# Thirty-two tokens' activations from gathered rows stand in the gate table, and each chunk of gate tables begins with three units without groups

## The reference

```python
def peer(h, w_query, sub_keys, u_emb, v_emb):          # h (1, 512, 2048)
    t = h.reshape(T, D)
    q = (t @ w_query).reshape(T, 8, 2, 128)
    s = jnp.einsum('thpk,pnk->thpn', q, sub_keys)      # scores against 2 x 128 sub-keys
    s_val, s_idx = lax.top_k(s, 16)
    cand = s_val[..., 0, :, None] + s_val[..., 1, None, :]
    cand_idx = s_idx[..., 0, :, None] * 128 + s_idx[..., 1, None, :]
    best, pos = lax.top_k(cand.reshape(T, 8, 256), 16)
    expert = jnp.take_along_axis(cand_idx.reshape(T, 8, 256), pos, -1)
    gate = jax.nn.softmax(best, -1)
    # per token: 8 heads x 16 = 128 experts of 16384, each one row of u_emb and of v_emb
    act = gelu(einsum('td,ted->te', t, u_emb[expert])) * gate
    return einsum('te,ted->td', act, v_emb[expert])
```

## Time and profile before

| | us |
|---|---|
| median of 3 runs | 3439.09 (3437.67 to 3448.2) |
| the profiled execution | 3448.69 |
| its span | 3446.8 |
| PE busy | 3374.7 (98% of the span) |
| POOL busy | 1849.8 (54%) |
| DVE busy | 2144.5 (62%) |
| ACT busy | 1186.6 (34%) |
| granted PE clock | 0.992 of full speed |

### The profile page before, as it was taken

The page is one execution under the profiler, slowest core; times in us unless marked ns, Lnnn a source line. Parts: engine busy times, 40 slices in busy tenths (PEclk is TensorE's granted clock), DMA queues, the critical chain, the costliest instruction groups (busy, mean ns, idle before and its releaser), DMA issues.

```text
span 3446.8 us, 44031 instructions
## 1 busy us (share of the span) xinstructions
PE 3374.7 (98%) x16931; PEld 2934.1 (85%) x16931; DVE 2144.5 (62%) x3280; ACT 1186.6 (34%) x1632; POOL 1849.8 (54%) x904
## 2 busy tenths in 40 slices
PE   7999999999999999999999999999999999999998
PEld 4688888766788899999999999999788888888887
DVE  2388887746414759993766676654566565566556
ACT  3322221234123232233555555543223233232223
POOL 1210001213444445776666666666788788787875
PEclk8999999999999999999999999999999999999999
DMA  9656642565423236777677767778978878878972
GB/s 384 255 185 205 218 165 107 182 225 205 160 98 147 88 126 243 287 270 277 256 315 301 293 268 299 313 312 320 354 281 349 335 295 336 345 290 327 357 270 108
DMA packets 184618, 874.71 MB, mean 254 GB/s; under 512 B 16621, under 2 KB 77501, under 8 KB 97844
## 3 DMA queue, kind: packets, MB, share of 16 engines
q1 hardware_dynamic: 122160, 525.38, 41.3%
q0 software_dynamic: 38688, 281.15, 20.3%
q10 hardware_dynamic: 23652, 66.69, 5.1%
HBM read 803.78 MB, written 69.32 MB: 253 GB/s over the span
## 4 chain that ended last, share of the span: by engine, by line
PE 90%; DVE 5%; DMA 3%; POOL 1%; ACT 1%; issue 0%; ACTq 0%; SPq 0%; DVEq 0%; POOLq 0%
PE bank L2120 84%; PE bank L2381 2%; DMA ring<-in_w_mod 1%; PE bank L2498 1%; PE bank L2355 1%; DMA ring<-in_v_emb 1%; POOL low L765 1%; PE bank L2128 1%; PE bank L2481 0%; DVE low L1436 0%; DMA rows_b<-in_v_rows,small 0%; DVE b L1880 0%; POOL split L807 0%; PE bank L2445 0%; DVE gate_w L1654 0%
## 5 line engine op out<-in xcount | busy, mean ns | idle before, releaser
L807 POOL TENSOR_TENSOR split<-ring,split 128x1024 fp32r<-128x1024 f32 x544 | 1356.7, 2504 | 650.8 <-ACT split L1145 650.0
L2120 PE MATMUL bank<-h_hi,split 128*128 128x384 f32 (+1 forms) x4608 | 1220.7, 341 | 6.9 <-POOL split L807 5.8
L1145 ACT ACTIVATE split<-ring 128x1024 fp32r<-128x1024 f32 x544 | 573.9, 1060 | 1418.2 <-PE bank L2120 1257.4
L2120 PE MATMUL bank<-split,a_split 128*128 128x512 f32 x4608 | 1047.6, 390 | 3.9 <-DVE acc L1992 2.3
L2120 PEld LDWEIGHTS bank<-split,a_split 128*128 128x128 f32 x4608 | 865.6, 188 | 185.6 <-DVE acc L1992 2.7
L2120 PEld LDWEIGHTS bank<-h_hi,split 128*128 128x128 f32 x4608 | 838.6, 188 | 27.8 <-POOL split L807 6.9
L2120 PE MATMUL bank<-h_lo,split 128*128 128x384 f32 (+1 forms) x2304 | 784.8, 341 | 0.0
L2120 PEld LDWEIGHTS bank<-h_lo,split 128*128 128x128 f32 x2304 | 433.2, 188 | 9.5
L2120 PE MATMUL bank<-hT_hi,w_hi 128*128 128x512 f32 (+1 forms) x768 | 289.5, 377 | 5.3 <-POOL ring_lo L727 2.2
L2120 PE MATMUL bank<-hT_lo,w_hi 128*128 128x512 f32 (+1 forms) x768 | 287.0, 374 | 0.0
L2120 PE MATMUL bank<-hT_hi,ring_lo 128*128 128x512 f32 (+1 forms) x704 | 260.4, 370 | 0.0
(11 more groups left out here) (318 smaller groups left out, 3858.2 us busy)
## 6 DMA issues: line engine op xcount, KB each, us to landing
ring<-in_u_emb SPq DMA_DIRECT2D x128, 1024.0 KB
ring<-in_v_emb SPq DMA_DIRECT2D x128, 1024.0 KB
ring<-in_w_mod SPq DMA_DIRECT2D x48, 1024.0 KB
ring<-in_w_in SPq DMA_DIRECT2D x44, 1024.0 KB
ring<-in_w_mod SPq DMA_DIRECT2D x64, 512.0 KB, 4.5
neurons<-tiny ACTq DMA_DIRECT2D x128, 192.0 KB
gate_table<-b ACTq DMA_DIRECT2D x6, 4096.0 KB, 15.1
weigh<-neurons SPq DMA_DIRECT2D x32, 768.0 KB
```

The source lines that it names most:

```text
L807: nc.gpsimd.tensor_tensor(split[:, r % 2, 1, at].bitcast(F32R), ring[:, r % 4, :, :].rearrange("p k n -> p (k n)")[:, at], split[:, r % 2, ...
L1145: nc.scalar.activation(split[:, q % 2, 0, at].bitcast(F32R), ring[:, q, :, :].rearrange("p k n -> p (k n)")[:, at], ACT.Copy)\
L2120: last = mm(out_, left[a].bitcast(F32R), right[b].bitcast(F32R), start=start and n == 0, stop=stop and n == 2)
```

## The change

1. Of the 384 dense tokens the last 32 (`EXTRA`) no longer go through the U sweep's matmuls: `neurons` moves 352 columns (TN). Their 32 x 128 activations come from gathered rows. A row tile has 128 partitions, so 4 slots of the 32 tokens are gathered at once: 32 gathers (`E_ROWS`, rows 58 to 89) for 128 slots.
2. The dots use one copy of h in PSUM. It is replaced twice by a load of 1 MB from DRAM and a copy on DVE: row 57 (`E_LOAD`, the 32 tokens' h four times) and row 90 (`T_LOAD`, the last tile's h again). So there are 162 rows before the V rows instead of 128. Both h arrays are stored to DRAM at the start by ACT.
3. The 32 tokens' Gelu value is multiplied into their gate before the gate table is built (U units 93 to 96; their part of the table is built in units 104 to 115), and the stored neurons hold a constant 1 in those 32 columns. The V sweep's matmuls stay as they are.
4. `GROUPS_AT` begins with three zeros; the groups stand closer after them.
5. The rows' places are a table, `ROW_UNIT`: one row a unit up to U unit 115, two a unit in 116 to 125, four at 126; the 25 left stand in V units 0 to 19 (one in even units, two in odd ones, none in each eighth), and the 128 V rows in V units 22 to 116, 1 or 2 a unit, none in each eighth. The V rows take turns in five buffers, two of them in the place of `x2_dense`, whose load (3 MB) moves from V unit 0 to V unit 118.
6. `h2_hi` and `h2_lo` are laid out in groups of 32 tokens instead of 128. ACT's V sweep is written out instead of looped. DVE waits for the h stores before the first search; the multiplications for the 32 tokens' h are two more operations on 32 partitions.

```diff
-GROUPS_AT = (0, 0, 2, 1, 2, 1, 2, 2, 1, 2, 1, 2)
+GROUPS_AT = (0, 0, 0, 2, 2, 1, 2, 2, 2, 1, 2, 2)
...
+def row_units():
+    at = list(range(3, PRE))
+    for unit in range(PRE, NK - 2):
+        at += [unit] * (2 if unit >= PRE + CHUNKS * CHUNK_UNITS else 1)
+    at += [NK - 2] * 4
+    unit = NK
+    while len(at) < U_ROWS:
+        if unit % 8 != 7:
+            at += [unit] * min(1 + unit % 2, U_ROWS - len(at))
+        unit += 1
+    units = [u for u in range(unit + 2, 2 * NK - 11) if u % 8 != 7]
+    return at + [units[m * len(units) // SLOTS] for m in range(SLOTS)]
...
             def gather_rows(n):
...
                 if n >= 3:
-                    pool.wait_ge(rows_used, n - 2)
-                pool.indirect_dma_start(gathered_rows[n % 3], None, u_rows[:, :] if n < SLOTS else v_rows[:, :],
...
+                    pool.wait_ge(rows_used, max(0, ROW_EARLIER[n]) + 1)
+                if n >= U_ROWS and ROW_COUNT[n] == 1:
+                    pool.wait_ge(split_used, 2 * V0)
+                rows, landed = gathered_rows[ROW_PLACE[n]], gathered[ROW_PLACE[n]]
+                if n in (E_LOAD, T_LOAD):
+                    pool.dma_start(rows, (extra_dram if n == E_LOAD else tile_dram)[:, :]).then_inc(landed, 16)
+                    return
...
-                if 0 <= r - (U0 + 2) < SLOTS:
-                    gather_rows(r - (U0 + 2))
-                for m in range(SLOTS):
-                    if V0 + 3 + m - m // 8 == r:
-                        gather_rows(SLOTS + m)
+                for n in range(ALL_ROWS):
+                    if U0 + ROW_UNIT[n] - (PRE <= ROW_UNIT[n] < NK - 12) == r:
+                        gather_rows(n)
...
-                nc.scalar.activation(neuron_out[:, q % 2, :], bank[:, 4 + q % 2, 0:TD], ACT.Gelu)\
+                nc.scalar.activation(neuron_out[:, q % 2, 0:TN], bank[:, 4 + q % 2, 0:TN], ACT.Gelu)\
...
             def dot(n):
...
+                if n in (E_LOAD, T_LOAD):
+                    dve.wait_ge(rows_used, n)
+                    rows = gathered_rows[ROW_PLACE[n]]
+                    nc.vector.tensor_copy(bank_rows[:, 0:D - P], rows[:, 0:D - P])
+                    nc.vector.tensor_copy(h2_last, rows[:, D - P:D]).then_inc(rows_used, 1)
+                    dve.wait_ge(rows_used, n + 1)
+                    return
...
-                dot(unit - 3)
+                dots(unit)
+                if unit == E_UNIT:
+                    dve.wait_ge(rows_used, T_LOAD)
+                    nc.vector.tensor_tensor(nval_e, nval_e, nval_last_e, ALU.add).then_inc(nval_summed, 1)
...
                     for k in range(h * 8, h * 8 + 8):
-                        last = mm3(bank[:, 4 + q % 2, 0:TD].rearrange("p (j t) -> p j t", t=P),
+                        last = mm3(bank[:, 4 + q % 2, 0:TN].rearrange("p (g t) -> p g t", t=EXTRA),
                                    [split[:, q % 2, w, k * P:(k + 1) * P] for w in range(2)],
-                                   [h2_hi[:, k, 0:JD, :], h2_lo[:, k, 0:JD, :]], k == 0, k == KT - 1)
+                                   [h2_hi[:, k, 0:TN // EXTRA, :], h2_lo[:, k, 0:TN // EXTRA, :]], k == 0, k == KT - 1)
```

More of the change, by code:

```diff
@@ L1318, in _ @@
                 finish_neurons(unit, unit % 4)
+                if unit == PRE + 1:
+                    act.wait_ge(idx_made, 5)
+                    for g in range(EG):
+                        act.dma_start(idx_e[g * EXTRA:(g + 1) * EXTRA, :], idx_part[:, g * EXTRA:(g + 1) * EXTRA])\
+                           .then_inc(e_moved, 16)
+                if unit == E_UNIT + 1:
+                    act.wait_ge(nval_summed, 1)
+                    nc.scalar.activation(nval_e, nval_e, ACT.Gelu).then_inc(nval_gelu, 1)
                 if k == CHUNK_UNITS - 1:
@@ L1897, in _ @@
             dve.wait_ge(score_copied, 1)
+            dve.wait_ge(e_moved, 16 * (EG + 1))
             sparse_search(0)
@@ L2038, in _ @@
             rest_group(1)
-            dot(NK - 4)
-            rows_added = 0
+            dot(first + 2)
+            dot(first + 3)
             for unit in range(NK):
```

176 lines of the change are left out of this document (124 added, 52 removed).

## The result

| | before | changed |
|---|---|---|
| median, runs on the same chip | 3440.81 us (3437.67 to 3448.2, 4 runs) | 3477.66 us (3473.15 to 3482.28, 4 runs) |
| ratio, 95% interval | | 1.0104 [1.0083, 1.0126] |
| span of the profiled execution | 3446.8 | 3476.6 |

The account below looks back on a forecast made before the run. PE was taken to bind the kernel, with transfers and POOL's list near. Terms -81.9 + 4 + 0 + 20 + 8 + 4 = -46 us from 3439.1 gave 3393 us; forecast 3378 to 3410 (0.5), range 3360 to 3430 (about 0.8).

Parts of the forecast that it names:

- The bound: Whole kernel: PE, busy 98% of the span, binds; the transfers and POOL's list are the near suppliers.
- The matmuls, -81.9: U sweep: 32 columns less save 13.3 ns at each of 6144 matmuls, 81.9 us; breaks between runs cost nothing.
- The rival: Matmuls don't get shorter: runs of 32 words cost 1.7 ns a break or more; 3463 us, chance 0.05.
- The search, +4: Search in the U sweep: gathers waiting for dots hold units back, 2.3 us more, plus 2 us at half clock.
- The chunks, 0: Gate chunks of the U sweep: 0 to 6 us lost over six chunks, taken as 0.
- the third empty unit: Gate chunks: puts the second group 27 us in instead of 19.2, after the store's landing; counted as nothing.
- The end of the U sweep, +20: Units 116 to 127: 46.4 MB take 118.6 us at 391 GB/s, PE needs 92.3; 20 us lost, between 5 and 35.
- the limit of 358 GB/s: A Trainium skill page's HBM limit per core; by it the border's 46.4 MB take 130 us, the sum 11 us higher.
- The V sweep, +8 and +4: V sweep: 8 us at its start from 25 late dots (0 to 20), 4 us later from crowded loads (0 to 40).
- twelve such places: V sweep: SP's 1.5 MB pieces ahead of the third unit's load, 13 to 15 us; 4 us over all twelve.
- The V sweep loses too: Rival: 26 us at the border, 10 behind it, 2 at each of twelve places; 3421 us, chance 0.17.
- the slower-than-before case: Rival, border and V sweep: transfers bind at 325 GB/s, from about 340 down; 32 us slower, 3471 us, chance 0.05.

Follow-up runs that it names:

- the two runs with one number of rows and 40 us apart in the V sweep: Dense-token h in one run, V rows in all units: paired rows clear of SP's pieces, 3482.92 us, or upon them, 3521.14 us.

## Why the prediction was wrong

- **The bound** was read rightly: PE, with POOL's list and the transfers near. The kernels that shortened only the matmuls lost nothing at the border.
- **The matmuls, -81.9: the step that failed first.** "a break between runs costs nothing that shows, and I take nothing for it" was taken from runs of 128 to runs of 32 words. The term measured -54.6. The line itself held (160.0 ns with one run). Eleven runs cost 4.4 ns at each of 6144 matmuls, 27 us. The rival named the right danger, but only as all or nothing, with 1.7 ns a break and a chance of 0.05; 0.4 ns a break takes a third of the gain.
- **The query stage: a missing term.** The sum gave the layout no price there, though it is read there too, in 16 runs: 11.4 ns x 768 = 9 us.
- **The search, +4:** the mechanism was right (idle of 11.6 us against the 8.1 worked out), the size was not. Against the kernel before, the idle is 5.8 us more where 2.3 were worked out, and the U matmuls between the stops, many of them at half clock, lose another 6 us (9.0 against 2.9 beyond their interval).
- **The chunks, 0:** hardly a PE gap (0.4 us), and the third empty unit is worth nothing, as said. They still lose 3 us against the matmuls' saving, and with the old list they lose next to nothing (614.6 instead of 617.1 us): the new list is most of it.
- **The end of the U sweep, +20:** right in size, 24.7, and in mechanism as far as the runs show. 46.3 MB moved where 46.4 were worked out, at 386 GB/s against 391. The traces go on to contradict the limit of 358 GB/s: 399 GB/s stand for 101 us in the run with fewer rows there. They fit another page of the Trainium skill: "Perfetto Trace Analysis", Roofline, says that a core whose pair is not active is bounded by its 16 DMA engines at some 435 GB/s.
- **The V sweep, +8 and +4: mis-sized, 37.** The stretch with the late dots cost 18 (8 taken, "0 to 20"), a stop of 6.1 us where the V rows begin among them. The rest was put at 4 us over "twelve such places", since 22.8 MB in 58 us left room. The place was the right one, the third unit's load behind the pieces, and the bounds of 0 to 40 held the 24 us. (The "11.6 us" read there run from the issue of a piece; the load itself took 10.2. From the piece on, "13 to 15 us" were forecast and 15.7 measured in the cycle shown.) What failed is that the room was judged by the mean: the two runs with one number of rows and 40 us apart in the V sweep show that a load is late when gathers and pieces come together, at a share of 0.87 where the faster one has 0.89.
- **The rivals.** "The V sweep loses too" had the mechanism, and the slower-than-before case was tied to a limit of 340 GB/s, which the windows with 386 and 399 GB/s rule out. None combined the V sweep's loss with a cost of the runs, and both came.
